# Masks added in the pass of the row minimum, forget-gate blocks turned, and the fill resequenced

## The reference, cut to what matters

```python
# latent attention, per block of 128 queries
s = (qn @ k_nope + qr @ k_rope) * scale
s = where(kpos <= qpos, s, NEG_INF); w = softmax(s); out = w @ v
# forget gates: c = cumsum(log_sigmoid(f + b_f))
s = (q @ k) * d ** -0.5 + c[q] - c[k]
s = where(kpos <= qpos, s, NEG_INF); w = softmax(s); out = w @ v
# sparse: keys from the indexer's top n_sel = 128
score = sum_h iw * relu(iq @ ik); top_val, top_idx = top_k(score, n_sel)
w = softmax(q @ k[top_idx]); out = w @ v[top_idx]
```

## Time and profile before

| what | before |
|---|---|
| median of 3 runs | 2200.23 us |
| profiled execution | 2201.58 us |
| its span, first to last instruction | 2199.6 us |
| busy: TensorE, VectorE, ScalarE, GpSimd | 2167.6, 1259.7, 916.8, 229.4 us |
| granted TensorE clock, share of full speed | 0.999 |
| DMA: moved, share of 16 engines | 196.03 MB on the main queue, 31.1% |

### The profile page before, as it was taken

One profiled execution on the slowest core, in us unless ns is written; L12 is line 12 of the kernel. 1 busy time (PEld: TensorE's weight loads), 2 busy tenths in 40 slices (PEclk: granted clock), 3 DMA queues, 4 the chain that ended last, 5 costly groups with the idle time before them and its releaser, 6 DMA issues. The chain is left out here.

```text
span 2199.6 us, 27868 instructions
## 1 busy us (share of the span) xinstructions
PE 2167.6 (99%) x10171; PEld 1734.5 (79%) x10173; DVE 1259.7 (57%) x2025; ACT 916.8 (42%) x1534; POOL 229.4 (10%) x164
## 2 busy tenths in 40 slices
PE   9999999999999999999999999999999999999998
PEld 7777788888778787788888787678778787888887
DVE  4676643343466665643343477388589678542554
ACT  4565443243355655443243264433543444222332
POOL 2000300001300001300001320143020230000000
PEclk9999999999999999999999999999999999999999
DMA  6113233333223431333233244124222232333231
GB/s 178 26 47 106 77 96 105 89 100 107 77 78 90 108 105 54 96 96 105 86 95 105 77 116 112 57 75 113 71 71 67 67 109 75 100 101 96 87 105 67
DMA packets 351556, 197.46 MB, mean 90 GB/s; under 512 B 21056, under 2 KB 340301, under 8 KB 351454
## 3 DMA queue, kind: packets, MB, share of 16 engines
q1 hardware_dynamic: 350882, 196.03, 31.1%
q10 hardware_dynamic: 316, 0.05, 0.0%
q0 software_dynamic: 256, 0.03, 0.0%
HBM read 193.93 MB, written 2.14 MB: 89 GB/s over the span
## 5 line engine op out<-in xcount | busy, mean ns | idle before, releaser
L376 ACT ACTIVATE WH<-RAW 128x1024 fp32r<-128x1024 f32 (+3 forms) x355 | 358.6, 1014 | 365.1 <-PE PB L414 271.6
L412 PE MATMUL PB<-XH,WH 128*128 128x512 f32 x1232 | 487.0, 395 | 4.0 <-DVE TG L3193 1.3
L414 PE MATMUL PB<-XH,WL 128*128 128x512 f32 x1232 | 480.2, 390 | 0.0
L413 PE MATMUL PB<-XL,WH 128*128 128x512 f32 x1232 | 479.6, 389 | 0.0
L392 DVE TENSOR_TENSOR WL<-RAW,WH 128x1024 fp32r<-128x1024 f32 x172 | 220.7, 1284 | 148.1 <-ACT WH L376 146.3
L412 PEld LDWEIGHTS PB<-XH,WH 128*128 128x128 f32 x1232 | 230.9, 187 | 57.1 <-issue 3.3
L414 PEld LDWEIGHTS PB<-XH,WL 128*128 128x128 f32 x1232 | 230.8, 187 | 49.6
L413 PEld LDWEIGHTS PB<-XL,WH 128*128 128x128 f32 x1232 | 231.0, 188 | 47.6 <-issue 0.7
L382 DVE TENSOR_TENSOR WL<-RAW,WH 128x1024 fp32r<-128x1024 f32 (+3 forms) x162 | 195.7, 1217 | 98.2 <-ACT WH L376 97.3
L412 PE MATMUL PB<-HH,WH 128*128 128x512 f32 x512 | 199.2, 389 | 0.0
L413 PE MATMUL PB<-HL,WH 128*128 128x512 f32 x512 | 199.2, 389 | 0.0
(11 more groups left out here) (539 smaller groups left out, 3620.8 us busy)
## 6 DMA issues: line engine op xcount, KB each, us to landing
RAW<-in_w_up SPq DMA_DIRECT2D x64, 512.0 KB, 4.0
RAW<-in_w_down SPq DMA_DIRECT2D x64, 512.0 KB, 3.8
RAW<-in_w_ffn_gate_up SPq DMA_DIRECT2D x44, 512.0 KB, 3.8
RAW<-in_w_gate SPq DMA_DIRECT2D x32, 512.0 KB, 4.0
RAW<-in_od_w_in SPq DMA_DIRECT2D x24, 512.0 KB, 6.9
RAW<-in_w_in SPq DMA_DIRECT2D x24, 512.0 KB, 4.0
RAW<-in_w_ffn_down SPq DMA_DIRECT2D x22, 512.0 KB, 3.3
RAW<-in_ple_w_gate SPq DMA_DIRECT2D x16, 512.0 KB, 4.1
```

What stands on the lines that cost most here:

```text
L376: act.activation(WH[:, s, 0:nb], RAW[:, s, 0:nb], ACT.Copy).then_inc(hi_done[s], 1)
L412: pe.matmul(PB[b][0:m, 0:n], WH[:, s, k, 0:m], rh[:, kk, :], start=kk == 0, stop=False)
L413: pe.matmul(PB[b][0:m, 0:n], WH[:, s, k, 0:m], rl[:, kk, :], start=False, stop=False)
L414: x = pe.matmul(PB[b][0:m, 0:n], WL[:, s, k, 0:m], rh[:, kk, :], start=False, stop=kk == last)
```

## The change

- Latent and sparse attention take the path of the fused add and minimum: `CAUSAL` (zeros, then the causal block, bf16) or `MSK` is added by VectorE, the sum goes to `SW` or `SWD`, and the exponential reads it there.
- Forget-gate attention takes its query blocks from the last to the first. GpSimd adds the causal mask in place to the diagonal block of `BC` ahead of each step; the mask products go.
- Order: in the mixer, query tile 1 is evacuated ahead of the normalisation (`mixer_early`), and the copies to `KM` stand at "uq" 0 and 2 instead of 0 and 1. `lin_pair` ends its first bank ahead of the second's last rounded part. Memory rows are turned at other places in `gate`. One gate part stands in front of memory attention's last values. In the indexer the first gate's tanh stands behind product 7. One selection round is later, and so is the mask. In the recurrence the cumulated logarithms lie in `FC`, tanh no longer waits for the scan, the sparse output's low part comes behind the first decay, and levels 7 and 8 and their fill are reordered. `first_hidden` takes the two gates before the two products.

```diff
@@ pe_scores
-                    pe.matmul(PB[2 + e][:, 0:w], q[:, qb * P:qb * P + P], keys_of[:, 0:w], start=part == 0, stop=False)
+                    x = pe.matmul(PB[2 + e][:, 0:w], q[:, blk * P:blk * P + P], keys_of[:, 0:w], start=part == 0, stop=part == 1)
+                done(x, "scores", ns[e])
...
-                        x = pe.matmul(PB[2 + e][:, 0:w], ID16[:], MSK[:, qb, 0:w], start=False, stop=True)
-                        x = pe.matmul(PB[2 + e][:, w - P:w], ID16[:], CA16[:], start=False, stop=True)
@@ dve_max (of all kinds but "mem")
+                    if kind == "fox":
+                        dve.wait_ge(sem["masked"], cnt.value("masked", (g, qb)))
+                    bias = {"swa": lambda: BIAS[:, h, lo:lo + w], "mla": lambda: CAUSAL[:, T - w:T],
+                            "fox": lambda: BC[:, g % 2, e, 0:w], "dsa": lambda: MSK[:, qb, 0:w]}[kind]()
@@ GpSimd, between the two layers' norms
+            for g in range(8):
+                for qb in range(TT):
+                    if qb == 0:
+                        pool.wait_ge(sem["decay_in" if g % 2 == 0 else "decay2_in"], 32 * (g // 2 + 1))
+                    else:
+                        for e in range(2):
+                            wait(pool, "biased", item("fox", 2 * g + e, qb - 1))
+                    blk = block_of("fox", qb)
+                    keys_of = BC[:, g % 2, :, blk * P:blk * P + P]
+                    done(pool.tensor_tensor(keys_of, keys_of, CA16[:].unsqueeze(1).to_broadcast([P, 2, P]), ALU.add), "masked", (g, qb))
@@ lin_pair
-                rounded(1, DT - 1)
                 wait(pe, names[1], (key, DT - 1))
                 low(0, DT - 1).then_inc(used[slots[0][0]], 1)
+                rounded(1, DT - 1)
@@ memory attention
+                fill = itertools.chain(gated(3), gated(1))
+                pe_attend(pe, ("mem",), 2, mem_between, lambda: lin1(8, XH, XL), lambda: next(fill))
@@ recurrence, TensorE
-                    if lv < 7:
-                        level_fill(9)
+                    level_fill(9 if lv < 7 else 3)
...
-                level_fill(9)
+                level_fill(8)
@@ gate
-                        if k == 4 and o in (3, 4):
-                            mem_turn(2 * o - 5)
+                        if o == 3 and k == 5:
+                            mem_turn(1)
+                        if o == 4 and k in (2, 7):
+                            mem_turn(2 + k // 7)
@@ forget-gate fill of the last pair
-                    for _ in range((4, 4, 3, 3)[qb]):
+                    for _ in range((4, 4, 3, 2)[qb]):
@@ ScalarE, mixer
-                    if what == "uq" and i < 2:
+                    if i in (0, 2):
                         act.wait_ge(sem["kr"], cnt.value("kr", "twice"))
-                        for h in range(4 * i, 4 * i + 4):
+                        for h in range(2 * i, 2 * i + 4):
                             x = act.activation(KM[64:128, h], KR[64:128, :], ACT.Copy)
-                        if i == 1:
+                        if i == 2:
                             done(x, "chain_a", "krope")
@@ ScalarE, indexer
-                    if r in (8, 17):
-                        gate_act(3, r // 8 - 1)
+                    if r in (7, 17):
+                        gate_act(3, r // 10)
@@ VectorE, mixer
+            def mixer_early(c):
+                if ENDED[c] and ENDED[c][0] == ("uq", 1):
+                    query_out(1)
@@ VectorE, behind sparse attention
-                dve_out(dve, "dsa", 1)
+                dve.wait_ge(sem["pv"], cnt.value("pv", pair_of("dsa", 1)))
...
                 decay(0)
+                lo_one(dve, N_GATE[2] + 1)
+                dve_out(dve, "dsa", 1)
+                lo_one(dve, N_GATE[2] + 2)
                 lo_one(dve, N_GATE[2] + 3)
@@ VectorE, levels
                     if lv == 7:
+                        merge(2, 7)
                         decay(8)
                         for q in range(28, 32):
                             keep(q)
+                        scale_by(8)
+                        keep(32)
+                        keep(33)
@@ VectorE, first gated MLP
+                    def first_hidden():
+                        for o in range(2):
+                            lin_ready(dve, st, 2 * o, 0, 4)
+                            done(dve.tensor_tensor(TG[:, o], PB[2 + 2 * o][:], RU[:], ALU.mult), "quad", 2 * o)
+                        lo_ahead(dve, st, 1, 0, 4)
...
```

More of the change, by code:

```diff
@@ L92 @@
  topk hsp hg_x hg_prod hg_read hg_e hg_d hg_o hg_small hx mn m2 varb ln_v x_full sum7q pj pj_free memsum cross xsum
- asum ysum h_up quad mvt yt yo ot_in xt_in z r_tok merge os brf vt off q_hi k_hi k_lo var_out var_in dn dn_free gain_in tok_ss tok_y tok_rt""".split()
+ asum ysum h_up quad mvt yt yo ot_in xt_in z r_tok merge os brf masked vt off q_hi k_hi k_lo var_out var_in dn dn_free gain_in tok_ss tok_y tok_rt""".split()
 def program(nc, known, t):
@@ L497, in pe_scores @@
                     for part, keys_of in enumerate(k):
-                        pe.matmul(PB[2 + e][:, 0:w], q[:, qb * P:qb * P + P], keys_of[:, 0:w], start=part == 0, stop=False)
+                        x = pe.matmul(PB[2 + e][:, 0:w], q[:, blk * P:blk * P + P], keys_of[:, 0:w], start=part == 0, stop=part == 1)
+                    done(x, "scores", ns[e])
                     continue
[L500 to L505, removed]
-                        x = pe.matmul(PB[2 + e][:, 0:w], ID16[:], MSK[:, qb, 0:w], start=False, stop=True)
-                    else:
-                        x = pe.matmul(PB[2 + e][:, w - P:w], ID16[:], CA16[:], start=False, stop=True)
-                    done(x, "scores", ns[e])
+                x = pe.matmul(PB[2 + e][:, lo:lo + w], q[:, blk * P:blk * P + P], k[:, ks[0] * P:ks[0] * P + w], start=True, stop=True)
+                done(x, "scores", ns[e])
         def pe_transposes(pe, kind, g, qb):
-            ks = keys(kind, qb)
+            ks = keys(kind, block_of(kind, qb))
             for e in range(2):
@@ L553, in steps_of, with pe_attend @@
             return [(kind, g, qb) for kind in kinds for g in range(n_pairs) for qb in range(TT)]
-        def pe_attend(pe, kinds, n_pairs, between=nothing, start=None):
+        def pe_attend(pe, kinds, n_pairs, between=nothing, start=None, ending=None):
             steps = steps_of(kinds, n_pairs)
@@ L618, in dve_normalise @@
                 n = item(kind, 2 * g + e, qb)
-                w = len(keys(kind, qb)) * P
+                w = len(keys(kind, block_of(kind, qb))) * P
                 st = STAT[:, 8 + 4 * (n % 4):12 + 4 * (n % 4)]
@@ L669, in act_attend, with dve_attend @@
             act_out(act, *steps[-1][:2])
-        def dve_attend(dve, kinds, n_pairs, between=nothing, last=True, start=None):
+        def dve_attend(dve, kinds, n_pairs, between=nothing, last=True, start=None, early=nothing):
             steps = steps_of(kinds, n_pairs)
@@ L1161, in _ @@
             done(pool.memset(STAT[0:64, 48:56], NEG), "zeroed", "relb")
+            done(pool.memset(CAUSAL[:, 0:T - P], 0.0), "zeroed", "causal")
             done(pool.memset(VROWS[:], 0.0), "zeroed", "vrow")
@@ L2401, in second_act @@
                     if c == 0:
-                        pairs(0, True)
+                        hi_ahead(act, st, 1, 0, 4)
+                        for o in range(2):
+                            act.wait_ge(sem["quad"], cnt.value("quad", 2 * o))
+                            act.activation(GT2[:, o], TG[:, o], ACT.Tanh, scale=0.5).then_inc(sem["gate_s"], 1)
+                        for o in range(2):
+                            act.wait_ge(sem["h_up"], hb + o + 1)
+                            act.activation(H2[:, o], HS2[:, 2 + o], ACT.Copy, scale=0.5).then_inc(sem["h_relu"], 1)
+                            hi_ahead(act, st, 2 + o, 0, 4)
                     if c == 1:
@@ L2584, in event @@
                 elif what == "uq":
-                    step()
-                    dve.tensor_tensor(QM[:, i], PB[b][:], RQ[:], ALU.mult).then_inc(evac[b], 1)
+                    if i != 1:
+                        query_out(i)
+                    lo_ahead(dve, st)
                     nxt()
@@ L2628, in event, with query_out @@
                     st.m += 1
+            def query_out(i):
+                b, ub = st.bank(0)
+                lin_ready(dve, st)
+                dve.tensor_tensor(QM[:, i], PB[b][:], RQ[:], ALU.mult).then_inc(evac[b], 1)
+            def mixer_early(c):
+                if ENDED[c] and ENDED[c][0] == ("uq", 1):
+                    query_out(1)
             skip()
@@ L2933, in second_dve @@
                 for c in range(2, 16):
-                    for _ in range({2: 0, 3: 2}.get(c, min(2 - c % 2, 16 - rnd))):
+                    for _ in range({2: 0, 3: 1}.get(c, min(2 - c % 2, 16 - rnd))):
                         select_round(rnd)
```

131 lines of the change are left out of this document (69 added, 62 removed).

## The result

The changed kernel takes 2187.53 us (median of 4 runs, 2187.15 to 2187.72) against 2200.4 of the kernel before in the same rounds: ratio 0.9939, 95% interval 0.9925 to 0.9954. Forecast were 2186.6 us and a range of 2182 to 2193. The profiled execution has a span of 2185.6 us, 14.0 less than before.

What follows compares the result with a forecast made beforehand. TensorE, busy 2167.6 of 2199.6 us, was taken as the bound. Gains, less 2.1 us at the rope copies and 0.2 for a longer memset, summed to 13.6 us: 2200.23 to 2186.6 us, range 2182 to 2193.

Steps and rivals of the forecast that it cites:

- 1. Masks: Causal masks off TensorE in latent, forget-gate and sparse attention: 1.8, 3.5 and 1.1 us, together 6.4 us won.
- 2. Query tile and copies: Mixer: early query tile evacuation gains 1.5 us, but TensorE waits for later rope copies; whole place costs 2.1 us.
- 3. Score banks: Latent attention: score bank is free once VectorE's sum is written, not after the exponential; 1.0 us won.
- 4. Turned blocks: Forget-gate blocks last to first: no stall at pair changes, GpSimd's masks hidden, waits at stage end mostly go; 0.9 us.
- 5. `lin_pair`: First bank ends 0.46 us earlier: nothing after ln1, 0.1 us twice after ln2, 0.45 at last projection; together 0.6 us.
- 6 and 7: Second layer's gate stage, memory rows turned later: 1.1 us; memory attention and index, gate part and earlier tanh: 1.4 us.
- 8. Recurrence: Recurrent branch: 0.5 us at L1551; reordered last levels and more filling remove waits at L1466 and L1569, 3.7 us.
- 9. First hidden tiles: First hidden tiles: the 1.3 us wait goes, 0.7 and 0.3 come back at the fifth tile; 0.3 us won.
- (a): Mixer: the rope copies hide and the early query tile gains; 4.0 us more, 2182.6 us; chance 0.12.
- (b): Work off one wait turns up at the next: half of 8.6 us in small gains given back, 2190.9 us; chance 0.17.
- (c): Only TensorE's removed mask work and the loss at the rope copies count: 4.3 us won, 2195.9 us; chance 0.06.
- (d): Forget-gate: GpSimd holds VectorE, the wide chain overruns at seven pair changes; slower, 2207.6 us with 3.0 overrun; chance 0.03.

Runs made afterwards that it cites:

- The kernel with the clock kept: Changed kernel plus 13 bf16 products that nobody reads, ahead of TensorE's wait for the rope copies; 2186.10 us.
- the repaired kernel: Changed kernel, first two head pairs awaiting only four rope copies, GpSimd's splits after the last level's scaling, two filling parts moved behind the recurrence's last products; 2181.68 us.

## Why the prediction was right, point by point

**The base.** The span fell by 14.0 us, the medians by 12.9: the profiled execution of before stood 1.2 us above the median of its later runs (1.35 was assumed), that of the changed kernel at its median. I had taken this distance as the same for both. So the span came out 0.4 us below its forecast (2186.0) and the median 0.9 above.

**1. Masks.** In the forget-gate stage 3.7 us by pair periods against 3.5. That GpSimd's share is hidden was right, with far more slack than argued. Sparse attention and L1551 together gave 1.8 (1.6).

**2. Query tile and copies.** The step that failed: 4.1 us lost instead of 2.1. Its mechanism was right: the copies ended at 125.99 (forecast 126.5), and the place cost 1.8 us at the first scores (2.1). The forecast priced the wait and took TensorE's speed behind it as given, a term put at nothing; the halved granted clock added 2.3 us. The kernel with the clock kept shows that share by itself, at 2.4.

**3. Score banks.** No wait at L506 for an exponential; latent attention gave 3.2 (2.8), its masks and the banks together; no run separates them.

**4. Turned blocks.** No stall at the changes of pair, as forecast. Outside the pairs 1.7 us instead of 0.9. By the distances between products the old order stalls TensorE at the stage's first value transposes (0.36), within the last block's transposes (0.56), behind the transposes of PIN (0.56) and at an output (0.30); the changed kernel only at the last (0.26). I had counted the two in the middle, by their waits of 0.7 and 0.4 in the earlier trace rows.

**5. `lin_pair`.** 0.45 at the last projection as forecast; behind the norms 0.8 instead of 0.2. After ln1 I had argued zero, since VectorE is in a split until 254.96. The changed kernel:

```profile
254.48 1.22 DVE L384 TENSOR_TENSOR WL<-RAW,WH 128x1024 fp32r<-128x1024 f32 x1
...
255.61 0.68 DVE L2722 TENSOR_SCALAR HR<-PB 128x512 f32<-128x512 f32 x1
...
256.35 0.50 PE L414 MATMUL PB<-XH,WH 128*128 128x512 f32 x1 [0.21 <-DVE HR L2722]
```

VectorE still goes from the split straight to the bank, but TensorE's wait is 0.2 instead of 0.3: the evacuation had not been bound by the split alone. It now starts 1.13 us behind the split's start instead of 1.25. The old order put back cost 0.14 here, so the gain is the order's.

**6 and 7.** 1.2 and 1.2 against 1.1 and 1.4. These parts, the sparse masks and part 9 had no experiment of their own; they rest on the two traces.

**8. Recurrence.** 2.7 instead of 3.7. The old wait at L1466 went, as forecast; of the one at L1569, which was to go as well, 0.5 us stayed. I gave back 0.3 for the split behind; in its place two other things came back. GpSimd's splits now fall on VectorE's scaling (0.8 us, shown by the kernel with the splits later). And two filling parts that used to lie between the last products and the first branch product (2 x 0.68) had been moved ahead, so the chain that makes YBL lay bare: 0.8 us and its restart, 1.1 together (shown by the last levels put back, and by the repaired kernel, where moving the two parts behind removes the wait). Without these two the gain would have been 2.7 + 0.8 + 1.1 = 4.6 us, more than the 4.0 counted: by the distances between products the two old waits had cost 2.3 and 2.1 us, not 2.0 each.

**9. First hidden tiles.** 1.1 instead of 0.3: the 1.3 us wait went, and of the 1.0 that I saw coming back at the fifth tile only 0.2 did.

**The rivals.** (a) was wrong as a sum, since the copies did not hide; with them hidden the kernel (2183.4) is near its 2182.6. (b), half of the small gains given back, did not come as a whole: the recurrence gave back 1.0 of 3.7, memory attention and index 0.2 of 1.4, and the other small parts gave what was forecast or more. (c) is excluded by the measured gains outside the masks. (d) is excluded by the masks added four times.

**The signs.** Of those that the forecast named, all came but two: 0.5 us stayed at L1569, and the wait after ln1 fell from 0.3 to 0.2. TensorE's idle time, 24.4 us, is under the 26 that would have proved it wrong; that sign could not see the slow products, which count as busy.

## What to carry to other kernels

Price a new wait of the bounding engine twice: its length, and what the granted clock does behind it, which the table by stretches shows. When filling work is moved to cover one chain, ask which later chain it covered before. And a semaphore for eight results, of which the next two heads need two, is a wait that can be split without moving anything.

## What the runs showed that I had not expected

The same wait costs differently from execution to execution. Behind the 3.5 us wait for the copies, the changed kernel lost 2.3 us to the halved clock in one execution and 1.1 in another (granted 0.50 and 0.51, then 0.60 and 0.84). Eight of the kept traces, of seven kernels that are alike up to there, have this wait. From the first latent scores to the same product behind them (at 131.64 us in the first trace) four of them took 5.5 to 5.7 us and four 4.4 to 4.6, against 3.2 in the kernel before and 3.1 with the clock kept.

Nor does a slow product always cost time. Behind a wait of 2.0 us in the recurrence the clock stayed at 1.00 in the kernel before and fell to 0.50 for 3.4 us in one execution of the kernel with the last levels put back; there the next wait took up the whole loss. Such a share belongs into a range, not into a sum, and it is to be read up to the next wait that remains.
